# Fourteen of 89 weight pieces loaded as two or three transfers of unequal row counts, in a gather-bound trunk

## What is computed

```python
def chunk(args):
    hh, ii, gg = args
    a = jnp.einsum('tkd,td->tk', u[ii], hh)
    w = gg * jax.nn.gelu(a)
    return jnp.einsum('tk,tkd->td', w, v[ii])
...
for i in range(DEPTH):
    h = rmsnorm(x, mix_norm[i])
    ...
    x = x + peer_mixer(rmsnorm(x, ffn_norm[i]), peer_wq[i], peer_keys[i], peer_u[i], peer_v[i])
    g = jax.nn.sigmoid((rmsnorm(x, ple_norm[i]) @ ple_wg[i]).astype(jnp.float32)).astype(x.dtype)
    x = x + g * (p[i] @ ple_wp[i])
return rmsnorm(x, final_norm)
```

## Time and profile before

| | |
|---|---|
| median of 3 runs | 2883.48 us (2882.32 to 2884.63) |
| profiled execution, its own time | 2884.08 us |
| span in the trace | 2882.3 us |
| mean granted TensorE clock | 0.912 |
| PE busy | 2265.8 us (79%) |
| DVE busy | 2143.5 us (74%) |
| POOL busy | 1282.7 us (45%) |
| ACT busy | 1072.4 us (37%) |
| moved by DMA | 1175.37 MB, mean 408 GB/s |

### The profile page before, as it was taken

How to read it: one execution, slowest core, us unless ns; L and a number is a source line. 1 busy time by engine, 2 the same in 40 slices (tenths; PEclk the granted TensorE clock), 3 DMA queues, 4 the chain that set the end, 5 groups by cost and what they waited for, 6 DMA issues and landing times.

```text
span 2882.3 us, 23329 instructions
## 1 busy us (share of the span) xinstructions
PE 2265.8 (79%) x6572; PEld 1170.4 (41%) x6572; DVE 2143.5 (74%) x4489; ACT 1072.4 (37%) x3181; POOL 1282.7 (45%) x1029
## 2 busy tenths in 40 slices
PE   6787667976978987888687898799967788666555
PEld 4444234522534553455253455346624433222112
DVE  6888768875797667757979766686696977677776
ACT  2443324333334333632323434364332334333222
POOL 2353543544434544533543443454444334555552
PEclk9899988988999998999898999999988999887877
DMA  9999999999999999999999999999999999999995
GB/s 363 420 399 420 419 421 401 417 420 420 419 408 412 380 420 420 419 420 420 408 420 384 416 374 419 421 419 420 420 398 420 419 420 420 420 420 420 420 421 216
DMA packets 164786, 1175.37 MB, mean 408 GB/s; under 512 B 18480, under 2 KB 19888, under 8 KB 23600
## 3 DMA queue, kind: packets, MB, share of 16 engines
q0 software_dynamic: 147456, 1073.81, 90.3%
q1 hardware_dynamic: 16624, 98.24, 8.4%
q10 hardware_dynamic: 576, 1.84, 0.2%
HBM read 1171.71 MB, written 2.10 MB: 407 GB/s over the span
## 4 chain that ended last, share of the span: by engine, by line
PE 36%; DMA 35%; DVE 18%; ACT 5%; issue 4%; POOL 2%; DVEq 0%; SPq 0%; ACTq 0%; POOLq 0%
DMA slot<-in_uv,idx 35%; PE acc L933 18%; DVE slot L1648 6%; DVE X L1639 3%; PE B L687 3%; PE B L605 3%; PE M L605 2%; POOL slot L582 2%; PE M L875 2%; PE M L687 1%; PE B L875 1%; ACT diag L1158 1%; DVE SD L1275 1%; DVE top_u L1280 1%; ACT A L948 1%
## 5 line engine op out<-in xcount | busy, mean ns | idle before, releaser
L933 PE MATMUL acc<-slot,diag 128*128 128x512 f32 x2904 | 1550.7, 673 | 580.9 <-ACT diag L1158 580.1
L582 POOL DMA_INDIRECT slot<-in_uv,idx x1024 | 1282.4, 1252 | 1555.3 <-PE acc L933 1076.4
L1648 DVE CUSTOM_DVE_ANT_0 slot<-slot,HP 128x1024 f32<-128x1024 f32 x1024 | 1243.3, 1221 | 564.2 <-DMA slot<-in_uv,idx 554.4
L933 PEld LDWEIGHTS acc<-slot,diag 128*128 128x128 f32 x2904 | 571.5, 210 | 1413.0 <-ACT diag L1158 853.7
L1150 ACT ACTIVATE act_a<-a 128x1 f32<-128x1 f32 x1024 | 206.6, 202 | 1616.7 <-DVE a L1648 1615.7
L1639 DVE SCALAR_TENSOR_TENSOR X<-slot,w,X 128x1024 f32<-128x1024 f32 x297 | 380.7, 1282 | 33.4 <-ACT w L1152 33.2
L1152 ACT ACTIVATE w<-act_a,gate 128x1 f32<-128x1 f32 x1024 | 301.5, 294 | 33.2
L1158 ACT ACTIVATE diag<-cst,w 128x128 f32<-128x128 f32 x726 | 291.7, 402 | 23.8
L687 PE MATMUL B<-TT,w 128*128 128x256 f32 (+1 forms) x448 | 88.8, 354 | 0.0
L687 PE MATMUL M<-TT,w 128*128 128x256 f32 (+1 forms) x448 | 88.3, 352 | 0.0
L687 PEld LDWEIGHTS B<-TT,w 128*128 128x128 f32 x448 | 78.3, 196 | 20.7 <-issue 13.1
(11 more groups left out here) (203 smaller groups left out, 1553.5 us busy)
## 6 DMA issues: line engine op xcount, KB each, us to landing
w<-in_wq SPq DMA_DIRECT2D x28, 1024.0 KB, 9.1
slot<-in_uv,idx POOLq DMA_INDIRECT x1024, 16.9
w<-in_ple_wg SPq DMA_DIRECT2D x8, 1024.0 KB, 9.1
w<-in_w_o SPq DMA_DIRECT2D x8, 1024.0 KB, 9.1
w<-in_w_dq SPq DMA_DIRECT2D x6, 1024.0 KB, 6.9
w<-in_w_uq_nope SPq DMA_DIRECT2D x8, 768.0 KB, 8.6
w<-in_ple_wp SPq DMA_DIRECT2D x5, 1024.0 KB, 14.2
slot<-in_wq SPq DMA_DIRECT2D x4, 1024.0 KB, 15.2
```

The costliest lines, as they stand in the source:

```text
L582: nc.gpsimd.indirect_dma_start(out=slot[s][:], out_offset=None, in_=uv[g // NC], in_offset=bass.IndirectOffsetOnAxis(ap=idx[:, g % HPB, k: ...
L933: last = nc.tensor.matmul(acc[:, half * 512:half * 512 + 512], diag[adds_on_pe(n) % DIAGS][:], slot[s][:, D + half * 512:D + half * 512 + ...
L1648: nc.vector.tensor_tensor_reduce(out=slot[s][:, 0:D], in0=slot[s][:, 0:D], in1=HP[:, g % HPB, :], scale=1.0, scalar=0.0, op0=ALU.mult, op1 ...
```

## The change

`PARTED` names fourteen pieces by number. Seven are loaded as 120 rows and then 8 rows, seven as 119, 7 and 2 rows. All parts of one piece count on the same semaphore, and `LANDINGS` gives PE the number of transfers after which a piece is complete. The order of the pieces, their places, the waits ahead of them and everything on the other engines stay.

```diff
+PARTED = {**{n: (120, 8) for n in (15, 25, 35, 47, 58, 72, 83)}, **{n: (119, 7, 2) for n in (17, 28, 45, 54, 66, 76,
+          81)}}
+
+def rows_of(n):
+
+    return PARTED.get(n, (P,))
+
+def landings():
+
+    counts, found = {}, []
+    for n, (where, h, _, _, there) in enumerate(HOMES):
+        if not there:
+            counts[where, h] = counts.get((where, h), 0) + len(rows_of(n))
+        found.append(counts[where, h])
+    return found
...
-                    sp.dma_start(places[where][h][:, 0:src.shape[1]], src).then_inc(w_loaded[where][h], 16)
+                    first = 0
+                    for count in rows_of(n):
+                        part = slice(first, first + count)
+                        sp.dma_start(places[where][h][part, 0:src.shape[1]], src[part, :]
+                                     ).then_inc(w_loaded[where][h], 16)
+                        first += count
...
-                where, h, loads, _, _ = HOMES[PIECES[name, g0, i]]
-                pe.wait_ge(w_loaded[where][h], 16 * (loads + 1))
+                n = PIECES[name, g0, i]
+                where, h, _, _, _ = HOMES[n]
+                pe.wait_ge(w_loaded[where][h], 16 * LANDINGS[n])
```

More of the change, by code:

```diff
@@ L294 @@
 HOMES = homes()
+PARTED = {**{n: (120, 8) for n in (15, 25, 35, 47, 58, 72, 83)}, **{n: (119, 7, 2) for n in (17, 28, 45, 54, 66, 76,
[9 more added lines that the diff above has]
+    return found
+LANDINGS = landings()
 STARTED = 3
```

## The result

The changed kernel takes 2982.1 us (median of 4 runs, 2980.9 to 2982.9) against 2883.1 us before in the same session: a ratio of 1.034, with a 95% interval from 1.032 to 1.036. It is 99 us slower, where 2 us less was forecast and the range ended at 2894 us.

What follows compares the result with a forecast made beforehand. DMA traffic at 420 GB/s was taken as the bound, with the slowest engine deciding; relief of that engine, less added rows and levelling, gave 2 us less than 2883.5 us: 2881.5 us, range 2869 to 2894 us.

Steps and rivals of the forecast that it cites:

- Rows per engine: In the fourteen pieces, equal shares: last engine 34.2 us less, first seven 23.9 us more, two of them 26.1 us more.
- The bound: Whole kernel: DMA bytes at a ceiling of 420 GB/s, 2798 us, 97% of the span; PE and DVE not near theirs.
- The last engine: At the gathers: the slowest engine decides when one has landed; instruction fetches put it 39.4 us over an engine without them.
- L: The DMA engine taken as last, getting every second q14 packet, 39 of 78, and losing 1.01 us each time.
- Leads: At drops in rate engines are levelled, so leads don't last; 13.3 us by totals shrinks to 4.2, then 2 us gained.
- rival 2: At three-part pieces: each bump of ten rows is paid, 3.1 us; three priced, 9.4 us slower, 2893 us; chance 0.13.
- Rival 1: Whole kernel: engines keep their leads and totals decide, 13.3 us faster, 2870 us; chance 0.22.
- rival 4: At the reshaped loads: transfers spread over all engines anyway, 2883.5 us; chance 0.07.
- Rival 3: At the reshaped loads: the last engine is among the first seven, 25 us slower, 2908.5 us; chance 0.08.
- PE's waits: PE's products on the pieces: later landing by 2.8 to 5.6 us stays covered, PE never waits, nothing added.
- The cover: At piece 76, the tightest three-part piece: 24 us from issue to first use less 9.1 to land leaves 14.8 us.
- SP and the fixed cost of transfers: SP's queue: 21 more issues of 0.33 us cost nothing; 2 us fixed per transfer, 42 us, overlaps and is left out.

Runs made afterwards that it cites:

- three_far: Only pieces 17, 45, 54 and 81 as 119, 7 and 2 rows, against the kernel before: 2924.9 us for 2884.0, 41.0 us slower.
- only_two: Only the seven two-part pieces (120 and 8 rows), the other seven single transfers again, against the kernel before: 2909.5 us for 2884.6.
- own_far: Pieces 17, 45, 54 and 81 whole, then 56 rows loaded again in 8 transfers of 7 rows 4 partitions apart, against the kernel before: 2896.8 us, 12.8 slower.
- experiment 4: three_far, three_near and own_far, testing lower DMA rate against PE's waits: 41.0, 29.9 and 12.8 us slower than the kernel before.
- three_near: Only pieces 28, 66 and 76 as 119, 7 and 2 rows, against the kernel before: 2913.9 us, 29.9 us slower.
- columns: All fourteen pieces as two transfers of 128 rows by half the columns, against the kernel before: 2885.5 us, 0.9 us slower.
- again_own: Seven three-part pieces loaded whole, then 56 rows again in 8 transfers of 7 rows 4 partitions apart, against the kernel before: 2919.5 us, 35.6 slower.
- evenodd: All fourteen pieces as two transfers of 64 rows, the even and the odd ones, against the kernel before: 2884.0 us, ratio 1.0003.
- halves: All fourteen pieces as two blocks of 64 neighbouring rows, against the kernel before: 2931.8 us, 47.2 us slower.

## Why the prediction was wrong

*The step that failed* is the first line of "Rows per engine" together with the price of a row: that a row costs its engine 0.311 us in whatever transfer it comes, so that only the count of rows matters. The division over 15, 8, 7, 7 and 2 engines was right. But the 0.311 us was read from transfers of 128 rows. With 119 rows the rate fell to 264 GB/s for 20 us, 7.4 us a piece; with the 3.1 us of the ten added rows this makes 10.5 us, and pieces 45 and 54 cost 10.7 and 10.4 us in `three_far` (9.9 us in the mean of seven). For 120 rows I had 1 row, 0.3 us; measured were 3.6 us. The term that the sum lacked is 7 x 7.4 us plus 7 x about 3.3 us, some 75 us. I wrote that no transfer of the trace has another row count, and bounded nothing from it: a form that the trace doesn't show should have had a price from both sides, and its slow side was open.

*The bound.* Right: the bytes' rate sets the time, and DVE's waits for gathers grew by 97 us when the rate fell.

*The last engine.* The 39.4 us of L rest on "every second q14 packet", taken from two places. The trace of the kernel before has 18 q14 packets after 2150 us, and only four steps of 3.5 us there in which DVE waits 2.2 us or more for rows (ending at 2409.16, 2482.86, 2708.36 and 2816.57 us), each with a q14 packet within 2 us. Four of 18 would make the term some 18 us; whether the others hit L unseen stays open, and no run tested it. Whether taking rows from that engine ever gains anything is open too, since each form tried that takes rows from it also disturbs the groups. `only_two`, 24.9 us slower, shows that any gain was below the price.

*Leads.* The prediction let most bumps of ten rows vanish in leads, and rival 2 priced three of seven. `own_far` has 8 rows more on seven engines at the full rate, and at pieces 45 and 54, where PE did not wait, it paid their 2.5 us in full. So no lead stood there to take them up. Rival 2's mechanism, each bump paid, was right; it accounts for about 22 us of the 99 if all seven paid, where it priced three pieces, 9.4 us.

*Rival 1* is excluded, *rival 4* too: 49 packets more, and landings far later. *Rival 3*, the last engine among the first seven, would have been 25 us and can't be told from here; it isn't needed.

*PE's waits.* "PE never waits" was wrong: four products waited 28.6 us in all. The largest is at piece 76, which took 24.8 us to land where 9.1 were known. The cover was misread as well. A piece of `w_o` has two products, M and B, and SP issued piece 76 at 1994.63 us (the row stands in the earlier trace rows), when PE had finished piece 74. Piece 75 then had two products, so the first of piece 76 is this one, and 2018.55 belongs to piece 77:

```profile
2008.21 3.62 PE L605 MATMUL M<-w,TT 128*128 128x256 f32 x16
```

It starts 13.6 us after the issue, so the cover was 4.5 us and not 14.8. The prediction's own 2.8 to 5.6 us of later landing would have used up most or all of it. In the changed kernel 24.8 us less 13.7 is the wait:

```profile
2092.86 5.81 PE L634 MATMUL M<-w,TT 128*128 128x256 f32 x16 [11.09 <-DMA w<-in_w_o]
```

In the mean it cost next to nothing of its own (experiment 4); piece 76 by itself set `three_near` back by 13.3 us, 2 to 3 us more than the pieces of `three_far`.

*SP and the fixed cost of transfers.* Right: 14 more transfers in `columns` cost 0.9 us. The 2 us for each further transfer, which the prediction named and left out of its sum, show in no run. The Trainium skill's rule against splitting ("Rules for kernel authors", 128 partitions and 1 MB per DMA) named the right form, and the number of transfers was not the reason.

What I should have read beside it: the Trainium skill's "DMA: Bandwidth & Descriptors", section "The descriptor swizzle", says that in a 128-partition transfer each engine writes the eight partitions of one memory port, and "SBUF — State Buffer", section "Door 1: The DMA port swizzle", gives the port by bits of the partition number. `again_own` agrees: seven engines with rows 4 partitions apart kept 418 GB/s, and neighbouring rows 264. The pages give the dealing for 128 rows alone; `evenodd`, at no cost, fits a 64-row form that keeps it.

## What to carry to other kernels

When DMA engines are the bound, look at which rows an engine carries, and so which partitions it writes, as well as at how many rows it has: 128-row loads and column splits of them ran at the full 420 GB/s beside the gathers, while loads of 120, 119, 64 or 7 neighbouring rows pulled all queues together down to between 243 and 264. A profile shows it as full DMA engines at a low rate, around the transfer and only there. At the one piece where DVE and PE were busy throughout, it cost nothing. Before a load is reshaped to balance engines, one piece in the new form, timed for its rate, tells more than a sum of rows.

## What the runs showed of the hardware that was not expected

- A weight load of 1 MB in the wrong form slows the other queue as well: in 9 us of `halves` the gathers moved 1.30 MB, in `evenodd` 2.73 MB.
- 64 even rows and 64 odd rows run like 128 (2884.0 us), two blocks of 64 don't (2931.8 us).
- Eight repeated rows on seven engines cost 2.5 us at pieces 45 and 54 at the full rate, their whole time, so a lead was worth nothing there.
- The slowing comes without idle engines: the DMA share stays at 1.01 to 1.03 while the rate drops by 37 to 42%.
